# First rounds, column sums between the blocks and last sums of a two-block fp32 kernel

## What is computed

```
x = x + merged @ w_out                       # first block: latent attention and a spatial gating unit
x = x + peer_ffn(rmsnorm(x) ...)             # experts: h @ peer_u, gelu, gate, @ peer_v
x = rmsnorm(x, g_final)
mod = silu(c) @ w_mod + b_mod                # second block: six rows sh1, sc1, g1, sh2, sc2, g2
h = rms_norm(x, norm1_g) * (1 + sc1) + sh1
x = x + g1 * (merged2 @ w_out_2)             # merged2: block attention and a state space branch
h2 = rms_norm(x, norm2_g) * (1 + sc2) + sh2
val, gt = split(causal_conv(h2 @ w_up), 2)
x = x + g2 * ((silu(gt) * val) @ w_down)
```

## Time and profile before

| | |
|---|---|
| runs | 3587.39, 3589.3, 3590.05 us; median 3589.3 |
| profiled execution | 3589.92 us, its span 3588.4 us |
| TensorE busy | 3573.2 us of the span |
| VectorE, ScalarE, GpSimd busy | 2693.5, 1784.2, 146.3 us |
| mean granted TensorE clock | 0.999 |

### The profile page before, as it was taken

The page is one execution under the profiler, slowest core; times in us unless marked ns, Lnnn a source line. Parts: engine busy times, 40 slices in busy tenths (PEclk is TensorE's granted clock), DMA queues, the critical chain, the costliest instruction groups (busy, mean ns, idle before and its releaser), DMA issues.

```text
span 3588.4 us, 50796 instructions
## 1 busy us (share of the span) xinstructions
PE 3573.2 (100%) x17792; PEld 3009.8 (84%) x17792; DVE 2693.5 (75%) x3504; ACT 1784.2 (50%) x2146; POOL 146.3 (4%) x213
## 2 busy tenths in 40 slices
PE   9999999999999999999999999999999999999999
PEld 7898888888888888888888888878888888888887
DVE  5664567668997877777788887899986667667668
ACT  5554444544444444444444445557764555555544
POOL 4000000000000000000000000010000000000000
PEclk9999999999999999999999999999999999999999
DMA  7445557766667988888887776755556565555554
GB/s 256 171 157 202 192 178 280 268 201 220 208 223 299 359 296 335 295 337 295 337 298 282 278 277 221 187 180 171 169 171 218 171 204 183 195 189 187 193 188 146
DMA packets 211073, 826.99 MB, mean 230 GB/s; under 512 B 24017, under 2 KB 25297, under 8 KB 197089
## 3 DMA queue, kind: packets, MB, share of 16 engines
q1 hardware_dynamic: 177904, 640.23, 52.6%
q10 hardware_dynamic: 15264, 102.99, 7.5%
q0 software_dynamic: 17744, 81.59, 6.2%
HBM read 786.43 MB, written 38.29 MB: 230 GB/s over the span
## 4 chain that ended last, share of the span: by engine, by line
PE 94%; DVE 3%; DMA 1%; issue 1%; ACT 1%; POOL 0%; SPq 0%; ACTq 0%; DVEq 0%; POOLq 0%
PE ps L2514 24%; PE ps L2516 24%; PE ps L2515 23%; PE ps L3214 9%; PE ps L3218 5%; PE ps L2890 2%; PE ps L2629 1%; PE ps L2631 1%; PE ps L2630 1%; DVE lo L1382 1%; PE ps L2923 1%; PE ps L2644 1%; DMA gate_scratch<-gst 0%; PE ps L3058 0%; PE ps L2559 0%
## 5 line engine op out<-in xcount | busy, mean ns | idle before, releaser
L728 ACT CAST hi<-raw 128x1024 fp32r<-128x1024 f32 x1216 | 1272.8, 1048 | 1681.1 <-PE ps L2516 1465.4
L1382 DVE TENSOR_TENSOR lo<-raw,hi 128x1024 fp32r<-128x1024 f32 x1214 | 1475.2, 1219 | 827.8 <-ACT hi L728 824.0
L2514 PE MATMUL ps<-hi,xx 128*128 128x512 f32 x2176 | 862.3, 396 | 3.0 <-DVE lo L1382 2.7
L2516 PE MATMUL ps<-hi,xx 128*128 128x512 f32 x2176 | 848.0, 390 | 0.0
L2515 PE MATMUL ps<-lo,xx 128*128 128x512 f32 x2176 | 847.4, 389 | 0.0
L2514 PEld LDWEIGHTS ps<-hi,xx 128*128 128x128 f32 x2176 | 408.7, 188 | 91.5 <-issue 7.8
L2516 PEld LDWEIGHTS ps<-hi,xx 128*128 128x128 f32 x2176 | 408.4, 188 | 86.6
L2515 PEld LDWEIGHTS ps<-lo,xx 128*128 128x128 f32 x2176 | 408.9, 188 | 81.4
L2514 PE MATMUL ps<-hi,Ph 128*128 128x512 f32 x1020 | 401.1, 393 | 0.2 <-DVE X L1865 0.2
L2516 PE MATMUL ps<-hi,Pl 128*128 128x512 f32 x1020 | 397.5, 390 | 0.0
L2515 PE MATMUL ps<-lo,Ph 128*128 128x512 f32 x1020 | 396.9, 389 | 0.0
(11 more groups left out here) (498 smaller groups left out, 3900.7 us busy)
## 6 DMA issues: line engine op xcount, KB each, us to landing
raw<-in_peer_u SPq DMA_DIRECT2D x256, 512.0 KB, 4.9
raw<-in_peer_v SPq DMA_DIRECT2D x256, 512.0 KB, 4.6
mraw<-in_w_mod ACTq DMA_DIRECT2D x96, 1024.0 KB, 7.4
raw<-in_w_up SPq DMA_DIRECT2D x176, 512.0 KB, 4.2
raw<-in_w_in SPq DMA_DIRECT2D x143, 512.0 KB, 3.7
raw<-in_in SPq DMA_DIRECT2D x128, 512.0 KB, 3.6
raw<-in_w_down SPq DMA_DIRECT2D x88, 512.0 KB, 4.1
raw<-in_out SPq DMA_DIRECT2D x64, 512.0 KB, 4.1
```

The costliest lines, as they stand in the source:

```text
L728: SC.copy(hi[:, n0 % SPL, 0:w], raw[:, n0 % RAW, 0:w]).then_inc(hi_ready, 1)
L1382: V.tensor_tensor(lo[:, n0 % SPL, 0:w], raw[:, n0 % RAW, 0:w], hi[:, n0 % SPL, 0:w].bitcast(F32), ALU.subtract).then_inc(lo_ready, 1)
L2514: PE_.matmul(acc, xhi[:, k0 + k, xs], H, start=s0, stop=False)
L2516: mm = PE_.matmul(acc, xlo[:, k0 + k, xs], H, start=False, stop=s1)
```

## The change

Three places are edited.

1. On ACT and DVE `split(j)` comes ahead of round j for j from 2 to 7. On PE round 2 moves from the middle of tile 1 to behind tile 0, with its wait for the third part of x; the `middle` argument goes.
2. `mod_sum` multiplies by 128 columns of ones instead of one. Sum k writes columns k to k + 127 of bank 4, and the next one overwrites all but the first of these; the sums are read from the same 16 columns as before. Ten sums become thirteen ahead of the first root's row, and three are left behind it.
3. `y_ready(2)` and `y_ready(3)` move from in front of the last UP sum to behind the last `flow`, each after two of the four tiles there.

```diff
--- before.py
+++ after.py
@@ -799,8 +799,11 @@
             act.wait_ge(raw_ready[0], 16)
             SC.copy(hi[:, 0, CH:TW], raw[:, 0, CH:TW]).then_inc(hi_ready, 1)
             for j in range(1, TC):
+                if j >= 2:
+                    split(j)
                 turn("h1", (j,), xh, scale=lambda k: C("g1", k))
-                split(j)
+                if j < 2:
+                    split(j)
             SC.activation(stat[:, 64:80], C("c", 0, KD), ACT.Silu).then_inc(csil, 1)
             for i in range(5):
                 act.wait_ge(x_in[i], 16)
@@ -2464,7 +2470,8 @@
             flow(FB - 2)
             for c in range(4):
                 rest(2)
-                y_ready(c)
+                if c < 2:
+                    y_ready(c)
             up_sum(FB - 1, 1, TOTAL - 16)
 
             conv_cols(FB - 1)
@@ -2476,7 +2483,9 @@
             product(FB - 1)
             rest(2)
             flow(FB - 1)
-            rest(4)
+            for c in range(2, 4):
+                rest(2)
+                y_ready(c)
             for c in range(4):
                 if c == 1:
                     rest(2)
@@ -2488,7 +2497,7 @@
 
         @block.tensor
         def _(pe):
-            def tile(n0, off, xhi, xlo, k0, banks, start, stop_, w=CH, ready=None, middle=None):
+            def tile(n0, off, xhi, xlo, k0, banks, start, stop_, w=CH, ready=None):
 
                 if not isinstance(n0, int) or n0:
                     pe.wait_ge(lo_ready, n0 + 1 + FIRST + off)
@@ -2514,8 +2523,6 @@
                         PE_.matmul(acc, xhi[:, k0 + k, xs], H, start=s0, stop=False)
                         PE_.matmul(acc, xhi[:, k0 + k, xs], L, start=False, stop=False)
                         mm = PE_.matmul(acc, xlo[:, k0 + k, xs], H, start=False, stop=s1)
-                    if middle is not None and k == 0:
-                        middle()
                 mm.then_inc(tile_used, 1)
 
             def last_tile(n0, xhi, xlo, k0, banks, first=None):
@@ -2577,19 +2584,15 @@
             def h1_ready(j):
                 pe.wait_ge(turn_lo, j + 1)
 
-            def h1_third():
-                pe.wait_ge(x_in[2], 16)
-                turn("h1", (2,), X)
-
             def h1_next(j):
-                if 0 < j < 6:
+                if j < 6:
                     if j % 2 == 0:
                         pe.wait_ge(x_in[j // 2 + 2], 16)
                     turn("h1", (j + 2,), X)
 
             for j in range(TC):
                 h1_ready(j)
-                tile(j, 0, xh, xl, SL * j, 0, j == 0, j == TC - 1, middle=h1_third if j == 1 else None)
+                tile(j, 0, xh, xl, SL * j, 0, j == 0, j == TC - 1)
                 h1_next(j)
             chunk(TC, 0, TC, 1, 0, xh, xl)
 
@@ -2902,8 +2905,7 @@
 
             def mod_sum(parts, bank, k0, k1):
                 for k in range(k0, k1):
-                    mm = PE_.matmul(ps[:, bank, k:k + 1], parts[:, k * P:(k + 1) * P], ones[:, 0:1],
-                                    start=True, stop=True)
+                    mm = PE_.matmul(ps[:, bank, k:k + P], parts[:, k * P:(k + 1) * P], ones[:], start=True, stop=True)
                 if k1 == KD:
                     mm.then_inc(mod_ps, 1)
 
@@ -3006,11 +3008,11 @@
             mod_sum(macc, 4, 0, 7)
             for r in range(6, 8):
                 grown_turn(r)
-            mod_sum(macc, 4, 7, 10)
+            mod_sum(macc, 4, 7, 13)
             pe.wait_ge(inv_ok, 1)
             pe.wait_ge(v_out, 8 * (NBLK - 1))
             row_of(INV, 6)
-            mod_sum(macc, 4, 10, KD)
+            mod_sum(macc, 4, 13, KD)
             pe.wait_ge(rstd_ready, ROOTS3)
             row_of(ROOT3 + 2, 7)
```

## The result

The changed kernel takes 3585.11 us (median of 22 executions, 3584.37 to 3585.78), the kernel before 3590.26 (22 executions on the same chip, 3587.21 to 3593.61). The ratio is 0.9987 [0.9981, 0.9993], so it is 5.15 us faster, less than the 0.2% that counted as a difference here. The forecast was a gain of 4.6 and 3584.7, in a range of 3582.3 to 3587.8. The profiled execution took 3584.37 with a span of 3582.8, 5.6 less than the span of before; the forecast of the gain, taken off that span, gives 3583.8.

What follows compares the result with a forecast made beforehand. The prediction took TensorE (PE), 94% of the chain that ended last, to bound the kernel. Beginning -1.9, between the blocks -2.8 and end +0.1 gave -4.6 us from the median 3589.3, so 3584.7, range 3582.3 to 3587.8.

Steps and rivals of the forecast that it cites:

- Beginning, before tile 2: Start of the kernel: weight cast and remainder ahead of the round bring tile 2 from 17.41 to 16.4, gain 1.0.
- Tiles 3 to 7: Later tiles of the beginning: gains of 0.25, 0.25 and 0.4; tile 7 at 32.0 against 33.95, beginning -1.9 in all.
- Rival 2: Beginning gives back: with tile 2's weight landing after 14.15 nothing is won there; -2.7, time 3586.6, chance 0.08.
- Sums of 128 columns, price 0: Column sums between the blocks: passes over 128 columns start 0.113 apart against 0.112 with one column, so no cost.
- Rival 3: Sum passes into each other's columns don't overlap, 0.275 each; -0.3 in all, time 3589.0, chance 0.03.
- Three more sums fill the root's wait: Between the blocks: twelve passes instead of six fill PE's wait of 0.68 for GpSimd's root; the row isn't late.
- The clock stays at 2.4 GHz: Between the blocks: PE keeps full clock, so the root's row takes 0.71 instead of 1.22.
- Rival 1: The clock falls between the blocks all the same; -2.9 in all, time 3586.4, chance 0.13.
- Between the blocks, -2.8: Tile 1 of the new block starts at 2241.15 instead of 2243.95, after a new PE wait of 0.7 for DVE.
- End, +0.1: Two y_ready moved behind the last convolution: 5.0 of DVE work covered by 5.7 of waits, cost 0.1.
- Rival 4: DVE's tail at the end: waits can't hide the two y_ready, last group 5.0 late; time 3589.6, chance 0.02.
- The sum: Whole kernel: beginning -1.9, between the blocks -2.8, end +0.1, together -4.6 us; time 3584.7, chance 0.68.

Runs made afterwards that it cites:

- order_only: Kernel before with only the new order on ACT and DVE; PE's transposes, sums and end as before; 3588.27 us, one execution.
- new_both: Changed kernel with the edits of new_shift and new_conv together; 3583.43 us (11 executions), ratio to before 0.9984.
- late_weight: Changed kernel with x's fourth part loaded ahead of weight tile 2, so that this tile lands later; 3586.45 us, one execution.
- c128_only: Kernel before with sums over 128 columns, still ten of them ahead of the root's row; 3587.09 us, one execution.
- p2_sums: Kernel before with both edits of the column sums alone (128 columns, thirteen ahead of the root's row); 3587.4 us (10 executions), ratio 0.9994.
- p3_yready: Kernel before with the edit of the end alone (two y_ready moved later); 3589.85 us (10 executions), ratio 0.9999.
- four_late: Changed kernel with all four y_ready behind the last convolution, each behind one remainder; 3588.89 us, one execution.
- after_again: The changed kernel once more, unedited, run beside three further variants; 3584.72 us (11 executions), ratio to before 0.9989.
- new_shift: Changed kernel with round 1's two shifts on DVE ahead of a half weight remainder between the blocks; 3584.56 us, one execution.
- new_conv: Changed kernel with ACT's base of the last convolution one cast earlier and DVE's first-half taps one remainder earlier; 3583.43 us (11 executions), ratio to before 0.9984.
- n13_onecol: Kernel before with thirteen one-column sums ahead of the root's row instead of ten; 3586.49 us, one execution.

## Why the prediction held, step by step

**Beginning, before tile 2: right in mechanism, and the term was mis-sized, 1.0 for 2.0.** The step took the landing of weight tile 2 from one execution, 13.15. That and order_only's are the latest of the landings in the thirteen rows with this order of loads, 12.15 to 13.15; kernels of the old and of the new order stand in both halves of them. The new order turns the landing into time: tile 2 starts 3.13 to 3.22 behind it in every row of that order but new_both, where PE itself comes to the tile only at 15.65, 0.35 behind the transposes. The old order doesn't: over the same landings tile 2 starts at 16.94 to 17.41, and in all five rows 3.81 or 3.82 behind the transposes of round 2 in the middle of tile 1, so it follows these. With the landing that the step assumed, order_only gives what it said. Over all rows with unchanged loads the small tile starts at 58.33 in the old order (mean of 5) and at 55.92 in the new one (mean of 8), a gain of 2.4. The changed kernel's 3.0 is this with its early landing, and the landing that the forecast took was by chance a late one, the changed kernel's by chance the earliest. The upper bound of 2.3 failed for another reason. It was the wait of 1.39 and 0.9 for the later tiles, as if PE came to tile 2 when it did before. The prediction gave the move of the transposes only a cost of 0.15, and no gain. In the changed kernel the last transposes ahead of tile 2 are at 14.93 instead of 15.42, and PE can be at the tile 0.35 behind them, 15.28, so up to 2.1 could be won there and 3.0 in all; and round 2, turned ahead of tile 1, is ready for an early landing. Tile 1 didn't start later by it, 12.09 for 12.13.

**Tiles 3 to 7: right.** Forecast 0.95 behind tile 2, measured 0.87 up to tile 7 (2.91 less 2.04). Rival 2 took the landing after 14.15 rightly as the point from which nothing is won before tile 2 (late_weight, 14.31), but it gave up this term too, and there 0.85 of it stayed: its price of 1.9 should have been about 1.0.

**Sums of 128 columns, price 0: right.** 14 passes up to the next instruction take 1.72 against 1.71, six 0.83 against 0.73 with the longer last pass, and c128_only loses nothing. The Trainium skill's table (TensorE: Matmul & The Clock Gate, section Back-to-back issue gap) has about 60 cycles for up to 64 columns and 134 for 128, from which the prediction had worked out 0.6 us; the trace doesn't agree with a difference of that size, 0.01 us in 14 passes. The prediction read the table for a case that it isn't for: the same section of the Trainium skill gives it for the gap of a matmul by itself, and says that in a stream the weight load sets the distance too. Here each pass has such a load, and the passes stand 0.11 us apart at either width. Rival 3 is out by the same rows.

**Three more sums fill the root's wait: right, and worth nothing once the clock is up.** The row starts 4.06 behind the first sum (2232.95 less 2228.89), and in c128_only, with the wait left, 4.05.

**The clock stays at 2.4 GHz: right**, in each of the 10, 22 and 11 executions listed. Rival 1 is out. By the Trainium skill (same page, Part 4: PE-mode transpose) a transpose doesn't count as busy in the way that a matmul does; whether it does can't be seen here, as the stretch with its transposes keeps its clock. Which of the two edits does it stays open: each alone went with a full clock, in one execution.

**Between the blocks, -2.8: right**, 2.82 between the two profiles. DVE started 4.81 behind the first sum (forecast 2236.5 less 2231.72, 4.78), the new wait is 0.43 and tile 1 is 9.41 behind the first sum, forecast 9.43. Over many executions this term isn't one number: with the old sums the stretch costs up to 4.1 us more than without the fall (13.49 less 9.4 in the block column), and by the spread of the times next to nothing in some. The 2.8 was read from one such execution; the medians of p2_sums give 2.3.

**End, +0.1: right**, +0.0 in the profiles, 0.19 in the medians of p3_yready and within their interval. The cover of 5.7 against 5.0 of work was counted rightly, as four_late shows: what was over, 1.1, is all that the second pair finds. Rival 4, whose price was the whole 5.0, is out.

**The sum.** -4.6 was forecast. The profiles give -5.6, of which 1.0 is the beginning's mis-sized term; the medians give -5.15 and, in the session of after_again, -4.36. The measured time, 3585.11, is nearer to the forecast of 3584.7 than either of its two parts: the median of before was 3590.26 over 22 executions, 1.0 above the 3589.3 of three that the forecast started from, and the gain was 0.55 larger. That the two misses work against each other is luck. The prediction's own range doesn't follow quite from its terms either: with 0.9 down to the lower bound of the beginning, 0.4 up to the higher, 0.1 and 0.7 it is 3583.5 to 3586.3, not 3583.3 to 3586.1. The measured time lies in both.

## What to carry to other kernels

An order of work that follows a load takes over the scatter of its landing, and one execution shows only one draw of it: price such a step from the landings of several runs, or as a slope behind the landing. An edit that looks like a cost only, like the moved transposes, can still set how early that load may be used. When a kernel's times scatter by more than the gain that you look for, list the granted clock of every execution before you explain the median. The stretch between the blocks here fell to the lower clock in most executions and not in the rest; with whole columns and the wait filled the mean clock was 1.000 in all of them, and the scatter went with the cost. Edits inside a run of an engine that has no gap, like new_shift, gained nothing here, while one that brought the first instruction of a run forward, like new_conv, did.

## What was not expected of the hardware

The landing of one and the same load, 512 KB issued at 4.65, came 7.5 to 8.5 us later over thirteen profiled executions. And the fall of the granted clock between the blocks isn't tied to one instruction. In the kernel before the root's row is slow already, 4.05 behind the first sum. The same PE instructions in p3_yready (first row, with 0.86 for six passes where rows 4 have 0.73) and in order_only (second row, 1.79 for twelve, where rows 4 have 2.56 and n13_onecol at full clock 1.40):

```profile
2234.49 0.86 PE L2908 MATMUL ps<-const,macc 128*128 128x1 f32 x6
```

```profile
2234.43 1.79 PE L2911 MATMUL ps<-const,macc 128*128 128x1 f32 x12
```

The first sum is at 2231.85 and 2229.83 there. So the fall began 2.6 to 3.5 behind it in the one execution and 4.6 to 6.4 behind it in the other.
